# Neighbourhood and sliding attention of one fused kernel: the sliding operands are written out between the neighbourhood items

## What is computed

```python
nq, nk, nv = (split_heads(a, NA_HEADS) for a in p[6:9])
y_na = neighborhood_attention(nq, nk, nv, nkc, nvc, na_rpb)
sq = apply_rope(split_heads(p[9], SWA_HEADS), cos, sin)
sk = apply_rope(split_heads(p[10], SWA_KV_HEADS), cos, sin)
sv = split_heads(p[11], SWA_KV_HEADS)
y_swa = sliding_window_attention(sq, sk, sv, skc, svc, swa_sink)
y = jnp.concatenate([y_gla, y_na, y_swa], axis=-1) @ w_out
```

## Time and profile before

| | |
|---|---|
| median of 3 runs | 3858.9 us (3856.09 to 3864.03) |
| profiled execution, its own time | 3861.16 us |
| its span in the trace | 3859.4 us |
| mean granted TensorE clock | 0.985 |
| TensorE matmul busy | 3722.8 us (96% of the span) |
| VectorE, ScalarE, GpSimd busy | 2394.9, 1576.6, 841.3 us |

### The profile page before, as it was taken

How to read it: one execution, slowest core, us unless ns; L and a number is a source line. 1 busy time by engine, 2 the same in 40 slices (tenths; PEclk the granted TensorE clock), 3 DMA queues, 4 the chain that set the end, 5 groups by cost and what they waited for, 6 DMA issues and landing times.

```text
span 3859.4 us, 56352 instructions
## 1 busy us (share of the span) xinstructions
PE 3722.8 (96%) x22665; PEld 3215.0 (83%) x22665; DVE 2394.9 (62%) x4154; ACT 1576.6 (41%) x2538; POOL 841.3 (22%) x695
## 2 busy tenths in 40 slices
PE   8999999989999999999999999998999999899998
PEld 5788777788898999999999999777777777677887
DVE  6455433466899668888888887567533345764333
ACT  4523343354335653333333335446422243653222
POOL 0112000153115354444334433010100000100000
PEclk9999999999999999999999999998999999899999
DMA  5211245533355669999999995220333432212332
GB/s 198 89 47 41 95 140 181 186 119 97 95 175 185 226 236 356 343 334 342 328 347 328 345 335 193 91 79 28 106 126 120 142 131 66 60 39 88 98 94 76
DMA packets 213908, 647.03 MB, mean 168 GB/s; under 512 B 19760, under 2 KB 65840, under 8 KB 210064
## 3 DMA queue, kind: packets, MB, share of 16 engines
q1 hardware_dynamic: 162816, 459.47, 36.1%
q0 software_dynamic: 50832, 183.95, 13.2%
HBM read 615.13 MB, written 27.79 MB: 167 GB/s over the span
## 4 chain that ended last, share of the span: by engine, by line
PE 83%; DVE 9%; ACT 4%; DMA 2%; issue 2%; POOL 0%; SPq 0%; DVEq 0%; ACTq 0%; POOLq 0%
PE ps L600 21%; PE ps L611 21%; PE ps L602 21%; PE ps L557 4%; PE ps L3495 2%; PE ps L2537 1%; PE ps L2564 1%; DVE hlo_plain L772 1%; PE ps L2555 1%; DMA raw<-w_in 1%; PE ps L902 1%; DMA raw<-peer_u 1%; ACT whi L524 1%; ACT l_NS L2587 1%; DVE wlo L532 1%
## 5 line engine op out<-in xcount | busy, mean ns | idle before, releaser
L600 PE MATMUL ps<-hhi,whi 128*128 128x512 f32 (+1 forms) x2824 | 1061.5, 377 | 5.4 <-DVE xres L3082 2.9
L532 DVE TENSOR_TENSOR wlo<-raw,whi 128x1024 fp32r<-128x1024 f32 x543 | 666.0, 1227 | 605.8 <-ACT whi L524 593.1
L602 PE MATMUL ps<-hlo,whi 128*128 128x512 f32 (+1 forms) x2824 | 1034.1, 367 | 0.2
L524 ACT ACTIVATE whi<-raw 128x1024 fp32r<-128x1024 f32 x616 | 648.8, 1054 | 597.2 <-PE ps L611 396.4
L611 PE MATMUL ps<-hhi,wlo 128*128 128x512 f32 (+1 forms) x2824 | 654.7, 370 | 0.0
L600 PEld LDWEIGHTS ps<-hhi,whi 128*128 128x128 f32 x2824 | 533.3, 189 | 106.5 <-issue 25.6
L602 PEld LDWEIGHTS ps<-hlo,whi 128*128 128x128 f32 x2824 | 532.2, 188 | 69.1 <-issue 4.1
L611 PEld LDWEIGHTS ps<-hhi,wlo 128*128 128x128 f32 x2824 | 500.5, 188 | 74.1 <-issue 6.8
L600 PE MATMUL ps<-ag_hi,whi 128*128 128x352 f32 x1024 | 328.7, 324 | 0.0
L602 PE MATMUL ps<-ag_lo,whi 128*128 128x352 f32 x1024 | 327.6, 321 | 0.0
L532 POOL TENSOR_TENSOR wlo<-raw,whi 128x1024 fp32r<-128x1024 f32 x74 | 181.6, 2462 | 166.0 <-ACT whi L524 164.0
(11 more groups left out here) (677 smaller groups left out, 6200.9 us busy)
## 6 DMA issues: line engine op xcount, KB each, us to landing
raw<-w_in SPq DMA_DIRECT2D x151, 512.0 KB
raw<-peer_u SPq DMA_DIRECT2D x128, 512.0 KB
raw<-peer_v SPq DMA_DIRECT2D x128, 512.0 KB
raw<-w_mod SPq DMA_DIRECT2D x96, 512.0 KB
raw<-w_gate SPq DMA_DIRECT2D x66, 512.0 KB
raw<-w_up SPq DMA_DIRECT2D x66, 512.0 KB
raw<-w_down SPq DMA_DIRECT2D x66, 512.0 KB
gate_dram<-stage SPq DMA_DIRECT2D x22, 1024.0 KB, 4.8
```

The costliest lines, as they stand in the source:

```text
L524: a.x.activation(whi[n % NW][:], raw[i % NRAW][:], ACT.Copy, bias=0.0, scale=1.0).then_inc(*a.gives("hi", i))
L532: e.x.tensor_tensor(wlo[n % NW][:], raw[i % NRAW][:], whi[n % NW][:].bitcast(F32), ALU.subtract).then_inc(*e.gives(*lo_sig(i)))
L600: t.x.matmul(o, w, p.hi, start=grp.opens and k == 0, stop=False)
L602: t.x.matmul(o, w, p.lo, start=False, stop=False)
```

## The change

- `attend` marks a tile as "valued" once its value matmuls are placed.
- `operands` of pair 2 wait, beside the four scores of pair 0, for the values of pair 1's first tile. All pairs' operands wait one short step more on TensorE, and their VectorE part comes one step behind the ScalarE part (the remainders).
- `window_operands`: the key's rotation (x = 3) waits for the operands of pair 1 and two steps more. The splits of the query pairs 0 and 1 now run in those steps, before the key's rotation, the third after the values' transposes, then the keys; VectorE's remainders are one step behind ScalarE. The wait for pair 2's last scores is gone.

```diff
--- before.py
+++ after.py
@@ -2565,6 +2565,7 @@
                                          start=j == 0, stop=j == n // 128 - 1)
                 ins.then_inc(*t.gives("attend_t", it.key, "out"))
                 note(t, "turn", it, False)
+                yield Mark(("valued", it.key))
                 if laying(t):
                     attended[it.m.name, it.out] = attended.get((it.m.name, it.out), 0) + 1
                     if attended[it.m.name, it.out] == m.NT:
@@ -2893,6 +2894,8 @@
             if i == 2:
                 for n in range(m.NT):
                     yield When(("swept", (m.name, 0, n)))
+                yield When(("valued", (m.name, 1, 0)))
+            yield 0.2
             yield 0.2
             yield 0.2
             yield Mark(("operands", m.name, i))
@@ -2908,8 +2911,10 @@
             for p in range(2):
                 ins = a.x.activation(nqd[hs[1 - p], p], q[hs[p]], ACT.Copy, bias=0.0, scale=1.0)
                 ins.then_inc(*(a.gives("opnd_a", m.name, i) if p else a.gives("opnd_a", m.name, i, "other")))
+            yield
 
         def vector(v):
+            yield
             idle(v)
             for p in range(2):
                 v.wait_ge("opnd_a", m.name, i, "q", p)
@@ -2935,6 +2940,10 @@
         def tensor(t):
             yield When((m.name, "normed"))
             for x in range(4):
+                if x == 3:
+                    yield When(("operands", m.name, 1))
+                    yield 0.2
+                    yield 0.2
                 yield When(("evac", place_of["proj", (m, *keys[x])], 0))
                 yield coming("lat", m.there(*keys[x]), ("c2", m.l))
                 b = take(t, "lat", (m.name, "rope", x), ("swaop_v", m.name, "sin", x))
@@ -2950,11 +2959,8 @@
                 ins = t.x.transpose(b[:, 128 * n:128 * n + 128], m.svT[:, 128 * n:128 * n + 128], ident)
             ins.then_inc(*t.gives("swaop_t", m.name, "value"))
             yield 0.3
-            yield When(("operands", m.name, 1))
-            yield When(("swept", (m.name, 2, 3)))
-            for _ in range(3):
+            for _ in range(2):
                 yield 0.2
-            yield 0.2
             for i in range(3, 6):
                 yield Mark(("operands", m.name, i))
 
@@ -2965,6 +2971,11 @@
                     v.x.tensor_tensor(m.sqs[i][hs[1 - p], p], xs[i][hs[p]], m.sqs[i][hs[p], p].bitcast(F32), ALU.subtract).then_inc(
                         *v.gives("swaop_v", m.name, "q", i, p))
             for x in range(4):
+                if x == 3:
+                    yield
+                    lower(0)
+                    yield
+                    lower(1)
                 if x:
                     v.wait_ge("swaop_v", m.name, "rope", x - 1)
                 v.wait_ge("swaop_t", m.name, "rope", x)
@@ -2978,9 +2989,8 @@
             v.x.tensor_copy(m.svtok[:].rearrange("p n f -> p (n f)"), held((m.name, "sv"))).then_inc(
                 *v.gives("swaop_v", m.name, "value"))
             yield
-            for i in range(3):
-                lower(i)
-                yield
+            lower(2)
+            yield
             for p in range(2):
                 v.wait_ge("swaop_a", m.name, "k", p)
                 v.x.tensor_tensor(m.skl[hs[p]], m.sk[hs[p]], m.skd[hs[p], p].bitcast(F32), ALU.subtract).then_inc(
@@ -2992,10 +3002,11 @@
                 ins.then_inc(*(v.gives("swaop_v", m.name, "keys") if p else v.gives("swaop_v", m.name, "far")))
 
         def scalar(a):
-            for x in range(4):
-                yield
-            yield
+            for x in range(3):
+                yield
             for i in range(3):
+                if i == 2:
+                    yield
                 a.wait_ge("swaop_v", m.name, "rope", i)
                 for j in range(2):
                     a.wait_ge("opnd_v", m.name, j)
@@ -3018,13 +3029,17 @@
                     ins = a.x.activation(dup[hs[1 - p], p], x[hs[p]], ACT.Copy, bias=0.0, scale=1.0)
                     ins.then_inc(*(a.gives("swaop_a", m.name, "keys") if p and what == "far" else
                                    a.gives("swaop_a", m.name, what, "other", p)))
+            yield
 
         def gpsimd(g):
             for x in range(4):
+                if x == 3:
+                    yield
+                    yield
                 g.wait_ge("swaop_t", m.name, "rope", x)
                 g.x.tensor_tensor(xs[x], xs[x], c2[:, COS:COS + T], ALU.mult).then_inc(*g.gives("swaop_g", m.name, x))
                 yield
-            for _ in range(5):
+            for _ in range(3):
                 yield
         return {"tensor": tensor, "vector": vector, "scalar": scalar, "gpsimd": gpsimd}
```

## The result

The changed kernel took 3874.97 us (median of 5 runs, 3871.96 to 3876.45) against 3858.9 (5 runs, 3855.22 to 3864.03): a ratio of 1.0042, interval 1.0031 to 1.0053. It is **16.1 us slower**. The forecast was 3861 with a range to 3873.

The account below looks back on a forecast made before the run. It took TensorE, busy 96% of 3859.4 us, as the bound. Two layers of 0.1 (neighbourhood) plus 1.0 (sliding) gave +2.2 us on the profiled 3861.16; with the median 2.3 below that, 3861 us, range 3846 to 3873.

Parts of the forecast that it names:

- Step 1: End of projection: lane 0's turn runs ahead of the last unit, where TensorE is full; 0.9 us later.
- Step 2: First waits: lane 1's turn no longer waits 2.77 us and starts at about 2583.6, not 2586.36.
- Step 3: Lane 2's first turn: after 9.3 us of VectorE's queue it comes at 2595.8, 4.5 us earlier.
- the meeting of remainder and multiply: VectorE's remainder beside GpSimd's key multiply: may add 0.96 us a layer, missed by 0.1 us; sum then +4.1.
- Steps 4 to 6: Neighbourhood attention: pair 1's scores after lane 2's values 5.8 us earlier, pair 2's first scores 2.2 later, last scores 6.1 later.
- each term counts twice: The second layer repeats the first within 0.1 us of TensorE work, so each layer's cost is doubled.
- Step 7: Tail from the last item's scores to `w_out`: 7.2 us instead of 13.2, so 6.0 us shorter.
- Sliding attention: Same TensorE work, but 36 more matmuls without spine cover: 0 to 2.1 us a layer, taken as 1.0.
- The clock: TensorE's clock after waits: 3.2 us per fall, one fall less or more per layer, 6.4 us in all either way.
- slower rival: Lane 0's last two items in a row: stage ends about 4 us later, 10 us in all, 3869 us; chance 0.26.
- The faster rival: Moved work hidden in VectorE's and ScalarE's idle time: 5 to 6 us a layer less, half gives 3849; chance 0.28.

Follow-up runs that it names:

- e11: The changed kernel without pair 2's wait for pair 1's first values, and with the operands' extra step for pair 2 only; 1.0 us faster than the kernel before.
- e3: The changed kernel without pair 2's wait for pair 1's first values; 0.1 us faster than the kernel before, ratio 1.0000.
- e7: The changed kernel with the key rotation's multiply on VectorE instead of GpSimd; 14.0 us slower than the kernel before.
- e9: The changed kernel, but lane 0 may not take the last item, so lane 3 takes it; 0.2 us slower than the kernel before, ratio 0.9995.
- e5: The kernel before with only pair 2's wait for pair 1's first values added; 5.4 us slower than the kernel before.
- e8: The changed kernel with pair 2 waiting for pair 1's first scores instead of its first values; 1.7 us faster than the kernel before.
- e12: The changed kernel with the keys' splits and the third remainder moved behind pair 2's operands; 3.8 us faster than the kernel before.
- e15: The changed kernel with e12's later splits, e9's rule for the last item and e8's wait; 2.4 us slower than the kernel before.
- e10: The changed kernel with e8's wait and e9's rule for the last item; 6.9 us faster than the kernel before.
- e1: The kernel before with only `window_operands` of the changed kernel; 3.2 us slower than the kernel before.

## Why the prediction was wrong

Seen from the end of the projection in layer one, us:

| | before | forecast | after |
|---|---|---|---|
| lane 1's turn | 4.5 | 1.0 | 1.6 |
| lane 2's first turn | 18.5 | 13.2 | 16.7 |
| lane 2's values | 23.8 | 18.7 | 22.0 |
| pair 2's first scores | 35.4 | 36.9 | 40.0 |
| last scores | 51.5 | 56.9 | 59.3 |
| `w_out` | 64.7 | 64.1 | 67.5 |

In layer one 6.6 us were lost where the forecast had 1.1: 0.9 more in step 1, 3.4 more in the stage, 1.0 more in sliding attention.

- **Step 1**, 0.9 us for the turn in the projection, was too small: about 1.8 (e11 against e3), and 1.8 and 2.8 for all that lies ahead of the stage in the two layers, 0.9 of the 2.8 near 3200 us.
- **Step 2** was right: the 2.77 us wait is gone. One of 2.22 us follows instead, ahead of the scores at 2588.03, where I had put about 1.2.
- **Step 3 is the step that failed.** I counted 9.3 us of VectorE's queue ahead of lane 2's first turn. It was 12.0, from 2586.48 to 2598.44. I had left out the remainder of the gated output that begins the queue, 1.2 us for its two halves, and the meeting of remainder and multiply, which "is missed by 0.1 us" by my walk, took place (0.97, e7). The queue also began 4.6 us after the end of the projection, and I had 3.8. VectorE, after:

```profile
2586.48 1.29 DVE L2367 TENSOR_TENSOR hlo<-l_tmp,hhi 128x512 fp32r<-128x512 f32 x2 [3.24 <-ACT hhi L2268]
...
2597.76 0.15 DVE L2652 RECIPROCAL l_st<-l_st 128x1 f32<-128x1 f32 x1
```

- **Steps 4 to 6** were right as distances in layer one. From lane 2's values to pair 2's scores I had 18.2 us and it took 18.0; from there to the last scores 20.0, and it took 19.3. They carried the 3.5 us of step 3 along. In layer two the last distance was 21.0, so that the last scores start at 61.3 us and `w_out` at 69.6: from pair 2's first scores on TensorE ran 7.7 us at 0.50 of its clock (3360.13 to 3367.83), in layer one 6.5 us at 0.59. That each term counts twice did not hold: layer one lost 6.6 us and layer two 10.2, of which 0.9 near 3200 us.
- **Step 7**: 7.2 us for the tail, 8.2 measured. The tail is 5.0 us shorter than before, as I had it in kind, but it starts 7.8 us later.
- **Sliding attention**: 1.0 forecast, 2.0 and 2.6 measured, by another cause. I had put it down to idle time with fewer spine matmuls for cover. Idle grew by 0.3 us only (7.38 to 7.66 in layer two). The rest is the clock, 0.94 and 0.95 against 0.98: behind the waits late in the stage the changed kernel shows 5 us at 0.66,

```profile
3445.00:3450.00 5.00, 3.70 (x36) 3.64 (x36) 2.65 (x11) 3.08 (x6) 0.00 (x0) 0.66 0.02 3
```

- **The clock** was put at half of 6.5 us per fall, with a gain as likely as a loss. Over the whole kernel TensorE's busy time grew by 8.3 us. In layer two 1.9 of it lie in the neighbourhood stage and 2.3 in the sliding one; in layer one the neighbourhood stage has 1.1 less and the sliding one 1.7 more.

The **slower rival** named the mechanism and its threshold: it "decides once the last scores start later than 2641". Corrected for the 1.8 us by which the changed run lies earlier, they start at 2643.0. It had 0.26 and a price of 3869, 6 us short. e9 shows its weight: the same kernel with company for the last item is as fast as the one before, so in this order the serial end costs 6.2 and 8.5 us in the two layers, not the 4 that I gave it. A serial end does not cost that everywhere: e5 has one too, and its stage is only 0.9 to 1.3 us longer than before; its last scores start at 54.2 us, not at 59 to 61. **The faster rival** was not idle either: in layer two the stages of e8, e9 and e12 are 3.5 to 5.7 us shorter than before. Their periods (730.71, 730.59 and 730.01 against 730.45) keep almost nothing of it; the projection and sliding attention take it back. Its price of 3849 us was also wrong as a sum: it takes the whole 5 us a layer off the kernel before, and half of it would be about 3854.

Left open: why e15 falls behind e10, why e5's serial end costs so much less, and how much of the 1 us or so by which sliding attention is longer in most variants comes from the new order and how much from the clock.

## What to carry over

Look at what runs beside the **last** item of a stage before you count the queue in the middle: here an item whose scores stood alone at the end cost more than a 7.6 us wait halfway (e1), and a rule of one line about who takes it was worth 15.9 us (e9). A wait in a planner is also an insertion point: the event just before it gives another order in three queues (e8), so try the neighbouring events. Where TensorE stands in short waits, count more than the idle time, since the work behind can run at a lower clock: in the whole kernel 7.0 us of added idle time came with 8.3 of added busy time, though not in every stage (layer one's neighbourhood stage had 3.8 more idle and 1.1 less busy).

## What the hardware showed that I had not expected

More busy time for the same matmuls is about half of the loss, 8.3 of 15.3 us. From the changed kernel to e10, layer two's neighbourhood stage shrinks by 12.7 us for the same 367 matmuls; 7.7 of these are TensorE's busy time (50.95 to 43.27), at a granted clock of 0.75 and 0.88, and only 5.1 are idle time.

The same order need not give the same clock. In e8 both layers have one order, and sliding attention takes 77.19 us at 0.98 in layer one, 78.39 at 0.96 in layer two:

```profile
2637.90:2715.09 77.19, 69.50 (x531) 55.98 (x529) 53.07 (x147) 43.35 (x97) 0.00 (x0) 0.98 0.09 28
3367.34:3445.73 78.39, 70.68 (x531) 57.21 (x529) 53.07 (x147) 43.37 (x97) 0.00 (x0) 0.96 0.09 28
```

The Trainium skill (TensorE: Matmul & The Clock Gate, Part 1: The HAM clock gate) says that the number of matmuls at the low clock changes from run to run of one kernel; here it changes between two layers of one run.

VectorE's remainder took 2.37 us beside GpSimd's multiply and 1.40 without it (e7), and GpSimd's multiply 1.68 in that place against the 1.28 of the earlier trace rows. The Trainium skill (SBUF — State Buffer, SBUF: two separate sides) calls the port that they share an exclusive lock for a whole instruction; the trace agrees: VectorE's second half, begun at 2594.74, took 1.65 us and not 0.69, and ended 0.55 behind GpSimd's multiply (2595.84).
